# Level products of a chunked linear attention: 64-partition operands replaced by 128-partition ones, with each head's decayed queries beside zeros

## The chip, the cores and the metric

The kernel runs on one core of one Trainium2 chip. The metric is the device time of one launch, in microseconds (us), as the median of several runs. The engines are TensorE (PE in the profile, with PEld its weight loads), VectorE (DVE), ScalarE (ACT), GpSimd (POOL) and SyncE (SP), each with its own instruction stream; they meet at semaphores.

## The reference, cut to what matters

One layer of a hybrid decoder block on 512 tokens of width 2048: adaLN modulation, one input projection, three groups of heads (pooling, gated linear attention, sparse attention), an output projection, and a SwiGLU FFN. Only the gated linear attention matters here. It has 4 heads, keys of 64 and values of 128 elements:

```
bc = cumsum(log_a)                                   # decay, per token and key element
att[i,j] = sum_d q[i,d] * k[j,d] * exp(bc[i,d] - bc[j,d])     for j <= i
out = att @ v + (q * exp(bc)) @ state
```

The kernel works in chunks of 128 tokens. The exponent of a difference can't be split into a factor for the query and one for the key without overflow, so the kernel splits the causal triangle of a chunk into levels: the diagonal (level 0), and then for each half-size h of 64, 32, ..., 1 (levels 1 to 7) all pairs whose key lies in the first half and whose query lies in the second half of a block of 2h tokens. For such a pair the decay is taken relative to the last token of the first half, and both factors are below one.

## The kernel before, in words

All weights are read as fp32, split by ACT and POOL into a high and a low part, and multiplied in three passes (line 347). The input projection comes first, then the linear attention, the pooling, the sparse attention, the output projection and the FFN. No other matmuls are placed beside the linear attention: PE, DVE and ACT hand its work back and forth.

Queries and keys lie transposed in `qkT`, `[128, 4, 512]`: planes 0 and 1 are the queries and planes 2 and 3 the keys. A plane holds two heads, the first in partitions 0 to 63, the second in partitions 64 to 127. `bb[1]` holds the cumulated decay in the same layout.

For level l DVE computes two differences into `ee` (lines 1078, 1079), ACT takes their exponent in place (line 776), and DVE multiplies the keys of the first halves into `kd` (line 1096) and the queries of the second halves into `qd` (line 1097). Each is one instruction over 128 partitions and 512 elements; the other halves of `kd` and `qd` stay zero, as memsets at lines 1041 to 1044 left them. There are two `qd` and two `kd` buffers, used in turn. The semaphore `lev_qk` then releases PE, which computes 16 products of 128 x 128 (`level`, line 478), four to each of four PSUM banks, and counts `lev_att` after each bank. DVE copies each bank into `att` under the level's mask (`copies`, line 1068). Each fp32 matmul appears in the profile as two MATMUL records, so a level has 32. The four products of a bank all take the same 64 partitions; banks 0 and 2 take partitions 0 to 63, banks 1 and 3 take partitions 64 to 127.

The order on DVE's queue is: differences of level l, `copies(l - 1)`, in the first four levels the reduction of a squared-norm tile at line 1084 (which releases POOL's next two instructions, lines 301 and 302), then the products for `kd` and `qd` of level l. So each level's matmuls wait for the copies of the level before them, and these wait for its matmuls.

Behind the levels `qd[0]` and `kd[0]` are filled once more with full 128-token decays (lines 1106, 1107); PE transposes `kd[0]` (line 495) and runs the sums over values and states (lines 506, 510, 518).

Of the kernel before, what the change touches and what calls it, by code (L numbers as in the profile page):

```python
# [13 lines left out]
P = 128  # L14
D = 2048
S = 512
# [28 lines left out]
ALU = mybir.AluOpType  # L45
# [23 lines left out]
def layer_kernel(nc, x, wstream, mstream, vecs, rows, grow_bias, tabs, cmp_tab, up, pool_w, w1, w2, out):  # L69
    with ExitStack() as ctx:  # L70
# [5 lines left out]
        def at(name, shape, dt=F32, offset=None):  # L76
            size = int(np.prod(shape[1:])) * 4
            if offset is None:
                offset = place[0]
                place[0] += -(-size // 32) * 32  # L80
            assert offset + size <= 229344, name
            return nc.alloc_sbuf_tensor_at(name, shape, dt, offset=offset)
# [27 lines left out]
        qkT = at("qkT", [P, 4, S], F32, pbase + 4 * T * 4096)  # L110
# [11 lines left out]
        place[0] = abase  # L122
        bb = [at(f"bb{i}", [P, 2, S]) for i in range(2)]
        ee = [at(f"ee{i}", [P, 2, S]) for i in range(2)]
        qd = [at(f"qd{i}", [P, 2, S]) for i in range(2)]
        kd = [at(f"kd{i}", [P, 2, S]) for i in range(2)]
        att = at("att", [P, T * LH, P])
        kdN = at("kdN", [P, T, 2 * P])
        state = at("state", [P, 2, 2 * P])
# [55 lines left out]
        ps = ctx.enter_context(nc.psum_tensor("ps", [P, 8, U], F32))  # L185
# [15 lines left out]
        lev_e, lev_exp, lev_qk, lev_att, lev_cp = sem("lev_e"), sem("lev_exp"), sem("lev_qk"), sem("lev_att"), sem("lev_cp")  # L201
# [141 lines left out]
        def _(pe):  # L343
# [96 lines left out]
            for k in range(KD):  # L440
                if k % 4 == 0:
                    pe.wait_ge(unit_ready, U_LG + k // 4 + 1)
                col = slice((k % 4) * 64, (k % 4) * 64 + 64)
                ins = passes(ps[0:64, 4, :], hmH[:, k, :], hmL[:, k, :], whi[:, k // 4, col], wlo[:, k // 4, col],
                             False, k == 0, k == KD - 1)
# [18 lines left out]
            for f in range(2):  # L464
                ins = nc.tensor.matmul(ps[:, f, :], upw[0:16, f * P:(f + 1) * P], lgT[0:16, :], start=True, stop=True)
            ins.then_inc(pe_gla, 1)

            for t in range(T):
                ins = nc.tensor.transpose(ps[:, 5, t * 64:(t + 1) * 64], lgT[0:64, t * P:(t + 1) * P], ident[0:64, 0:64])
            ins.then_inc(pe_gla, 1)  # L470

            def level(l, q_, k_):

                for n in range(4):
                    p0 = (n % 2) * 64
                    for c in range(4):
                        tok = slice((2 * (n // 2) + c // 2) * P, (2 * (n // 2) + c // 2 + 1) * P)
                        ins = nc.tensor.matmul(ps[:, 4 * (l % 2) + n, c * P:(c + 1) * P], k_[p0:p0 + 64, c % 2, tok],  # L478
                                               q_[p0:p0 + 64, c % 2, tok], start=True, stop=True)
                    ins.then_inc(lev_att, 1)  # L480

            pe.wait_ge(dve_gla, 1)
# [10 lines left out]
            for t in range(T):  # L493
                for f in range(2):
                    ins = nc.tensor.transpose(ps[:, t // 2, (t % 2) * 256 + f * P:(t % 2) * 256 + (f + 1) * P],
                                              kd[0][:, f, t * P:(t + 1) * P], ident[:, :])
# [3 lines left out]
            for t in range(T):  # L500
                if t:
                    pe.wait_ge(st_ready, t)
                for f in range(2):
                    if t:

                        nc.tensor.matmul(ps[:, t, f * 256:(f + 1) * 256], qd[0][:, f, t * P:(t + 1) * P], state[:, f, :],
                                         start=True, stop=False)
                    for h in (2 * f, 2 * f + 1):
                        a_h = att[:, 8 * (t // 2) + 4 * (h % 2) + 2 * (t % 2) + f, :]
                        ins = nc.tensor.matmul(ps[:, t, h * P:(h + 1) * P], a_h,  # L510
                                               proj[:, t, 512 + h * P:512 + (h + 1) * P],
                                               start=t == 0, stop=t == 0 or h % 2 == 1)
                ins.then_inc(o_psum, 1)
                if t < T - 1:
                    for h in range(LH):
                        f, p0 = h // 2, (h % 2) * 64
                        v_h = proj[:, t, 512 + h * P:512 + (h + 1) * P]
                        ins = nc.tensor.matmul(ps[p0:p0 + 64, 4 + t, h * P:(h + 1) * P], kdN[:, t, h * 64:(h + 1) * 64],
                                               v_h, start=True, stop=True)
                    ins.then_inc(st_psum, 1)  # L520


            for g in range(4):
                pe.wait_ge(dve_gla, 3)
                u_g = slice(g * P, (g + 1) * P)
                for t in range(T):
                    first = ptab[:, 3 * g + (0 if t == 0 else 1), :]
                    ins = nc.tensor.matmul(ps[:, g, t * P:(t + 1) * P], proj[:, t, u_g], first, start=True, stop=t == 0)
                    if t:
                        ins = nc.tensor.matmul(ps[:, g, t * P:(t + 1) * P], proj[:, t - 1, u_g], ptab[:, 3 * g + 2, :],  # L530
                                               start=False, stop=True)
                ins.then_inc(pool_pe, 1)
            for g in range(4):
                pe.wait_ge(pool_act, g + 1)
                nc.tensor.matmul(ps[:, 4 + g, :], poolw[:, g * P:(g + 1) * P], poolD[:, g, :],
                                 start=True, stop=True).then_inc(pool_pe, 1)


            for v in range(2):
                pe.wait_ge(c_dup, v + 1)  # L540
                for g in range(G):
# [4 lines left out]
                    for t in range(T):  # L546
                        ins = nc.tensor.transpose(ps[:, g, t * P:(t + 1) * P], dup[:, t, g * P:(g + 1) * P], ident[:, :])
# [6 lines left out]
                for i in range(16):  # L554
                    pe.wait_ge(c_gt, 16 * v + i + 1)
                    for m in range(2):
                        ins = nc.tensor.matmul(ps[:, 4 + m, 0:P], w1s[:, i, m * P:(m + 1) * P], gt[:, i, :],  # L557
                                               start=i == 0, stop=i == 15)
                ins.then_inc(c_hid, 1)
                pe.wait_ge(c_hsaved, v + 1)  # L560
                if v == 0:
                    for m in range(2):
                        ins = nc.tensor.matmul(ps[:, 6, 0:DH], hid[:, m, :], w2s[:, 0, m, :], start=m == 0, stop=m == 1)
# [4 lines left out]
                else:  # L568
                    for g in range(G):
                        pe.wait_ge(c_act, g + 1)  # L570
                        for m in range(2):
                            ins = nc.tensor.matmul(ps[:, 6 + g % 2, 0:DH], hrep[:, m, :], w2s[:, 1, m, :],
                                                   start=m == 0, stop=m == 1)
# [5 lines left out]
            with pe.Fori(0, G) as g:  # L579
                pe.wait_ge(n_qk, g + 1)  # L580
                pe.wait_ge(o_saved, 4 * g + 4)
                for a in range(2):
                    for t in range(T):
                        ins = nc.tensor.transpose(ps[:, a, t * P:(t + 1) * P], qn[:, t, a * P:(a + 1) * P], ident[:, :])
                    ins.then_inc(n_tr, 1)
                for b in range(2):
                    for t in range(T):
                        ins = nc.tensor.transpose(ps[:, 3 + b, t * P:(t + 1) * P], kn[:, t, b * P:(b + 1) * P], ident[:, :])
# [48 lines left out]
                for n in range(NU):  # L637
                    t, r, b = units[n]
# [17 lines left out]
            for k in range(4, KD):  # L656
# [3 lines left out]
                for t in range(T):  # L660
                    ins = nc.tensor.transpose(ps[:, k % 8, t * P:(t + 1) * P], proj[:, t, c0:c0 + P], ident[:, :])
# [10 lines left out]
            for k in range(KD):  # L672
                if k >= 8:
                    pe.wait_ge(f_ready, k - 7)
                for t in range(T):
                    ins = nc.tensor.transpose(ps[:, k % 8, t * P:(t + 1) * P], xn[:, t, k * P:(k + 1) * P], ident[:, :])
# [270 lines left out]
        def _(dve):  # L947
# [90 lines left out]
                                   op0=ALU.mult, op1=ALU.min).then_inc(dve_gla, 1)  # L1038
            V.memset(att[:, :, :], 0.0)
            V.memset(state[:, :, :], 0.0)  # L1040
            V.memset(qd[0][:, :, :], 0.0)
            V.memset(qd[1][:, :, :], 0.0)
            V.memset(kd[0][:, :, :], 0.0)
            own(V.memset(kd[1][:, :, :], 0.0))

# [24 lines left out]
            for l, hs in enumerate(LEVELS, 1):  # L1070

                e = ee[l % 2][:, :, :].rearrange("p f s -> p (f s)").rearrange("p (n a s) -> p n a s", a=2, s=hs)
                b = bc.rearrange("p (n a s) -> p n a s", a=2, s=hs)
                nb = 2 * S // (2 * hs)
                ref = b[:, :, 0, hs - 1:hs].to_broadcast([P, nb, hs])
                if l >= 2:
                    dve.wait_ge(lev_qk, l - 1)
                V.tensor_tensor(e[:, :, 0, :], ref, b[:, :, 0, :], ALU.subtract)
                V.tensor_tensor(e[:, :, 1, :], b[:, :, 1, :], ref, ALU.subtract).then_inc(lev_e, 1)
                copies(l - 1)  # L1080
                if l <= T:

                    dve.wait_ge(qk_sq, l)
                    V.tensor_reduce(qr[:, (l - 1) * NH:l * NH], nsq[:, :].rearrange("p (h d) -> p h d", d=DH),
                                    AX.X, ALU.add).then_inc(qk_sum, 1)
                if l == T + 1:
                    dve.wait_ge(qk_sum, T)
                    V.tensor_scalar(qr[:, :], qr[:, :], 1.0 / DH, EPS, ALU.mult, ALU.add).then_inc(qk_var, 1)
                dve.wait_ge(lev_exp, l)
                if l >= 3:  # L1090
                    dve.wait_ge(lev_att, 4 * (l - 2) + 4)
                qv = qkT[:, 0:2, :].rearrange("p f s -> p (f s)").rearrange("p (n a s) -> p n a s", a=2, s=hs)
                kv = qkT[:, 2:4, :].rearrange("p f s -> p (f s)").rearrange("p (n a s) -> p n a s", a=2, s=hs)
                qo = qd[l % 2][:, :, :].rearrange("p f s -> p (f s)").rearrange("p (n a s) -> p n a s", a=2, s=hs)
                ko = kd[l % 2][:, :, :].rearrange("p f s -> p (f s)").rearrange("p (n a s) -> p n a s", a=2, s=hs)
                V.tensor_tensor(ko[:, :, 0, :], kv[:, :, 0, :], e[:, :, 0, :], ALU.mult)
                V.tensor_tensor(qo[:, :, 1, :], qv[:, :, 1, :], e[:, :, 1, :], ALU.mult).then_inc(lev_qk, 1)

            b = bb[1][:, :, :].rearrange("p f (t s) -> p (f t) s", t=T)
            e = ee[0][:, :, :].rearrange("p f (t s) -> p (f t) s", t=T)  # L1100
# [2 lines left out]
            V.tensor_tensor(e, b[:, :, P - 1:P].to_broadcast([P, 2 * T, P]), b, ALU.subtract).then_inc(lev_e, 1)  # L1103
            copies(7)
            dve.wait_ge(lev_exp, 8)
            V.tensor_tensor(qd[0][:, :, :], qkT[:, 0:2, :], ee[1][:, :, :], ALU.mult)
            V.tensor_tensor(kd[0][:, :, :], qkT[:, 2:4, :], ee[0][:, :, :], ALU.mult).then_inc(lev_qk, 1)
            for t in range(T - 1):
                dve.wait_ge(st_psum, t + 1)
# [307 lines left out]
```

## Time and profile before

| | us |
|---|---|
| median of 3 runs | 2764.28 (2763.25 to 2765.51) |
| the profiled execution, its own time | 2766.02 |
| its span, first to last instruction | 2764.2 |
| PE busy (share of the span) | 2541.9 (92%) |
| DVE busy | 1060.8 (38%) |
| ACT busy | 850.5 (31%) |
| POOL busy | 1057.2 (38%) |

PE's busy time counts overlapping records once. Line numbers are those of the kernel before. The granted clock (PEclk) is 1.00 at 2.4 GHz and 0.50 at 1.2 GHz.

### The profile page before, as it was taken

To read this page: it belongs to the slowest core of one execution; us is meant where nothing else is said; L and a number is where in the kernel's file an instruction comes from. 1 tells how busy PE (TensorE), PEld (TensorE's weight loads), DVE (VectorE), ACT (ScalarE), POOL (GpSimd) and SP (SyncE) were. 2 spreads that over 40 slices of the span, in tenths; PEclk is the share of its full clock that TensorE was granted. 3 is DMA by queue.
4 is the path that set the end of the run, shared out by engine and by line. 5 is a ranking of instruction groups with operands and counts; after the bars stand their busy time and mean duration, and the time that the engine had idled before them with its cause. 6 is when DMAs were issued, how large, how long until landed. Compare 5 with 4: busy or idle time off the path is not lost.

```text
span 2764.2 us, 35964 instructions
## 1 busy us (share of the span) xinstructions
PE 2541.9 (92%) x11497; PEld 2070.3 (75%) x11497; DVE 1060.8 (38%) x1626; ACT 850.5 (31%) x1571; POOL 1057.2 (38%) x816
## 2 busy tenths in 40 slices
PE   5699999956479999997999999999999999999998
PEld 4677778845367777876888888888888888888887
DVE  4756777767334552113131222222222313131404
ACT  3032222221255653323323222222222222222222
POOL 0034445521300002442444444444444444444444
PEclk9999999975778999998999999999999999999999
DMA  9837777720200003221222222222222222222233
GB/s 335 271 134 259 272 273 274 269 103 0 78 1 1 0 0 114 91 91 51 94 92 94 96 91 91 98 91 91 99 91 91 94 95 91 94 96 91 91 99 121
DMA packets 86615, 318.57 MB, mean 115 GB/s; under 512 B 9632, under 2 KB 10288, under 8 KB 85040
## 3 DMA queue, kind: packets, MB, share of 16 engines
q1 hardware_dynamic: 84672, 306.44, 32.5%
q10 hardware_dynamic: 1904, 11.62, 1.1%
q8 instruction: 24, 0.39, 0.1%
q14 instruction: 15, 0.12, 0.0%
HBM read 313.82 MB, written 4.19 MB: 115 GB/s over the span
## 4 chain that ended last, share of the span: by engine, by line
PE 89%; DVE 6%; ACT 2%; DMA 2%; issue 1%; ACTq 0%; DVEq 0%; SPq 0%
PE ps L347 75%; PE ps L597 3%; PE ps L626 3%; PE ps L615 1%; PE ps L478 1%; DMA modw<-in_mstream 1%; DVE macc L987 1%; PE ps L557 1%; DVE macc L989 1%; PE ps L604 1%; PE ps L410 1%; PE ps L401 1%; DMA xin<-in_x 0%; PE ps L394 0%; DVE dtmp L1281 0%
## 5 line engine op out<-in xcount | busy, mean ns | idle before, releaser
L289 POOL TENSOR_TENSOR wlo<-raw,whi 128x512 fp32r<-128x512 f32 x744 | 1004.0, 1350 | 1400.5 <-ACT whi L706 1400.5
L706 ACT ACTIVATE whi<-raw 128x512 fp32r<-128x512 f32 x744 | 469.7, 632 | 1493.8 <-PE ps L347 1488.9
L347 PE MATMUL ps<-hfH,whi 128*128 128x512 f32 x1408 | 559.4, 397 | 5.0 <-DVE hfull L1291 5.0
L347 PE MATMUL ps<-hfL,whi 128*128 128x512 f32 x1408 | 559.1, 397 | 0.0
L347 PE MATMUL ps<-hfH,wlo 128*128 128x512 f32 x1408 | 559.0, 397 | 0.0
L1307 DVE TENSOR_TENSOR hfull<-gsil,ps 128x512 f32<-128x512 f32 x44 | 30.3, 688 | 893.2 <-PE ps L347 449.9
L347 PEld LDWEIGHTS ps<-hfH,whi 128*128 128x128 f32 x1408 | 265.9, 189 | 70.2 <-DVE hfull L1291 5.4
L347 PEld LDWEIGHTS ps<-hfL,whi 128*128 128x128 f32 x1408 | 265.9, 189 | 64.7
L347 PEld LDWEIGHTS ps<-hfH,wlo 128*128 128x128 f32 x1408 | 265.8, 189 | 64.9
L347 PE MATMUL ps<-wlo,huH 128*128 128x512 f32 x704 | 280.8, 399 | 0.0
L347 PE MATMUL ps<-whi,huL 128*128 128x512 f32 x704 | 277.5, 394 | 0.0
L347 PE MATMUL ps<-whi,huH 128*128 128x512 f32 x704 | 276.1, 392 | 0.0
L969 DVE SCALAR_TENSOR_TENSOR macc<-modw,cact,macc 128x512 f32<-128x512 f32 x240 | 263.9, 1100 | 12.9 <-DMA modw<-in_mstream 3.1
L347 PE MATMUL ps<-whi,hmH 128*128 128x512 f32 x512 | 204.7, 400 | 0.0
L347 PE MATMUL ps<-wlo,hmH 128*128 128x512 f32 x512 | 204.1, 399 | 0.0
L347 PE MATMUL ps<-whi,hmL 128*128 128x512 f32 x512 | 201.9, 394 | 0.0
L1321 DVE TENSOR_TENSOR dtmp<-ps,grow 128x512 f32<-128x512 f32 x176 | 121.8, 692 | 205.6 <-PE ps L347 189.4
L1323 DVE TENSOR_TENSOR x<-x,dtmp 128x512 f32<-128x512 f32 x176 | 182.8, 1039 | 6.0
L347 PEld LDWEIGHTS ps<-whi,huL 128*128 128x128 f32 x704 | 132.1, 188 | 34.3
L347 PEld LDWEIGHTS ps<-whi,huH 128*128 128x128 f32 x704 | 132.2, 188 | 31.7
L347 PEld LDWEIGHTS ps<-wlo,huH 128*128 128x128 f32 x704 | 132.2, 188 | 30.5
L347 PEld LDWEIGHTS ps<-whi,hmL 128*128 128x128 f32 x512 | 96.1, 188 | 26.1 <-issue 1.9
(243 smaller groups left out, 2704.3 us busy)
## 6 DMA issues: line engine op xcount, KB each, us to landing
raw<-in_wstream SPq DMA_DIRECT2D x372, 512.0 KB, 3.3
modw<-in_mstream SPq DMA_DIRECT2D x192, 512.0 KB, 4.9
xin<-in_x SPq DMA_DIRECT2D x4, 1024.0 KB, 8.3
w1s<-in_w ACTq DMA_DIRECT2D x2, 2048.0 KB, 7.8
x<-in_x ACTq DMA_DIRECT2D x4, 1024.0 KB, 8.7
out_y<-x SPq DMA_DIRECT2D x16, 256.0 KB, 3.2
grow<-in_grow_bias SPq DMA_DIRECT2D x1, 2048.0 KB, 18.5
cmpb<-in_cmp_tab ACTq DMA_DIRECT2D x1, 1024.0 KB, 9.7
```

What stands on the lines that cost most here:

```text
L289: nc.gpsimd.tensor_tensor(wlo[:, s, :], raw[:, r, :], whi[:, s, :].bitcast(F32), ALU.subtract).then_inc(unit_ready, 1)
L347: ins = nc.tensor.matmul(acc, lhs, rhs, start=first and n == 0, stop=last and n == 2)
L401: ins = nc.tensor.matmul(ps[:, 4 + j, 0:1], macc[:, j * P:(j + 1) * P], ones[:, 0:1], start=j >= 2, stop=True)
L410: ins = nc.tensor.transpose(ps[:, k % 4, t * P:(t + 1) * P], xin[:, t, k * P:(k + 1) * P], ident[:, :])
L478: ins = nc.tensor.matmul(ps[:, 4 * (l % 2) + n, c * P:(c + 1) * P], k_[p0:p0 + 64, c % 2, tok], q_[p0:p0 + 64, c % 2, tok], start=True, st ...
L597: nc.tensor.matmul(ps[:, n % 3, 0:w], qT[:, r // 2, t * P:(t + 1) * P], kz[:, 2 * b + r % 2, 0:w], start=True, stop=True).then_inc(s_psum, 1)
L626: ins = nc.tensor.matmul(ps[:, 5 + t % 2, b * 256 + r * DH:b * 256 + (r + 1) * DH], pT[:, n % 2, c * P:(c + 1) * P], v_b, start=c == 0, st ...
L706: A(whi[:, k % SPLIT, :], raw[:, k % 8, :], ACT.Copy).then_inc(unit_hi, 1)
L969: ins = V.scalar_tensor_tensor(out=macc[:, :], in0=src, scalar=scal, in1=macc[:, :], op0=ALU.mult, op1=ALU.add)
L1307: V.tensor_tensor(hfull[:, c, :], gsil[:, c, :], ps[:, 4 * a + 2 + c, :], ALU.mult).then_inc(up_saved, 1)
L1321: own(V.tensor_tensor(dtmp[:, t % 2, :], ps[:, 4 * (c % 2) + t, :], grow[:, D + 512 * c:D + 512 * (c + 1)], ALU.mult))
L1323: V.tensor_tensor(x1[:, t, col], x1[:, t, col], dtmp[:, t % 2, :], ALU.add).then_inc(y_added, 1)
```

## The change

For levels 1 to 7 the queries get two buffers for each parity in place of one: `qd[i][0]` holds decayed queries in partitions 0 to 63 and zeros in 64 to 127, `qd[i][1]` the other way round. The product at line 1097 becomes two instructions over 64 partitions each. The matmuls of levels 1 to 7 take all 128 partitions of the keys and of one of the two query buffers; the zeros cancel the other head of the plane. Level 0 stays with 64 partitions. The memsets at the start clear four `qd` buffers in place of two, and the last full product of the queries goes to `bb[0]`, which is free by then.

```diff
-        qd = [at(f"qd{i}", [P, 2, S]) for i in range(2)]
+        qd = [[at(f"qd{i}{a}", [P, 2, S]) for a in range(2)] for i in range(2)]
...
-                        ins = nc.tensor.matmul(ps[:, 4 * (l % 2) + n, c * P:(c + 1) * P], k_[p0:p0 + 64, c % 2, tok],
-                                               q_[p0:p0 + 64, c % 2, tok], start=True, stop=True)
+                        if l == 0:
+                            lhs, rhs = k_[p0:p0 + 64, c % 2, tok], q_[p0:p0 + 64, c % 2, tok]
+                        else:
+                            lhs, rhs = k_[:, c % 2, tok], q_[n % 2][:, c % 2, tok]
+                        ins = nc.tensor.matmul(ps[:, 4 * (l % 2) + n, c * P:(c + 1) * P], lhs, rhs,
+                                               start=True, stop=True)
...
-                        nc.tensor.matmul(ps[:, t, f * 256:(f + 1) * 256], qd[0][:, f, t * P:(t + 1) * P], state[:, f, :],
+                        nc.tensor.matmul(ps[:, t, f * 256:(f + 1) * 256], bb[0][:, f, t * P:(t + 1) * P], state[:, f, :],
...
-            V.memset(qd[0][:, :, :], 0.0)
-            V.memset(qd[1][:, :, :], 0.0)
+            for i in range(2):
+                for a in range(2):
+                    V.memset(qd[i][a][:, :, :], 0.0)
...
-                V.tensor_tensor(qo[:, :, 1, :], qv[:, :, 1, :], e[:, :, 1, :], ALU.mult).then_inc(lev_qk, 1)
+                for a in range(2):
+                    half = slice(a * 64, (a + 1) * 64)
+                    ins = V.tensor_tensor(qo[a][half, :, 1, :], qv[half, :, 1, :], e[half, :, 1, :], ALU.mult)
+                ins.then_inc(lev_qk, 1)
...
-            V.tensor_tensor(qd[0][:, :, :], qkT[:, 0:2, :], ee[1][:, :, :], ALU.mult)
+            V.tensor_tensor(bb[0][:, :, :], qkT[:, 0:2, :], ee[1][:, :, :], ALU.mult)
```

## Rows read from the trace of the kernel before

**Rows 1.** The page: the chain that ended last, by engine.

```profile
PE 89%; DVE 6%; ACT 2%; DMA 2%; issue 1%; ACTq 0%; DVEq 0%; SPq 0%
```

**Rows 2.** The chain in time (start us, us, what): before the levels.

```profile
597.01 0.67 DVE qd L1041
...
598.09 0.91 DVE qd L1042
...
599.16 0.91 DVE kd L1043
...
600.24 0.92 DVE kd L1044
601.18 1.24 DVE bb L1047
```

**Rows 3.** The chain in time: matmuls of levels 1, 2, 6 and 7.

```profile
620.31 5.14 PE ps L478 x32
...
630.78 5.15 PE ps L478 x32
...
664.38 5.14 PE ps L478 x32
...
669.59 0.58 issue
670.17 0.68 DVE kd L1096
670.85 0.61 DVE qd L1097
...
671.50 5.14 PE ps L478 x32
```

**Rows 4.** Timeline of POOL and DVE, 576 to 622 us (start us, us, engine, line, op).

```profile
578.16 1.89 POOL L301 TENSOR_TENSOR nsq<-proj 128x1024 f32<-128x1024 f32 x1
...
617.87 2.38 DVE L1097 TENSOR_TENSOR qd<-qkT,ee 128x512 f32<-128x512 f32 x1
620.29 1.41 DVE L1078 TENSOR_TENSOR ee<-bb 128x512 f32<-128x512 f32 x1
621.62 0.68 DVE L1079 TENSOR_TENSOR ee<-bb 128x512 f32<-128x512 f32 x1
...
617.43 2.27 POOL L301 TENSOR_TENSOR nsq<-proj 128x1024 f32<-128x1024 f32 x1 [36.39 <-DVE qr L1084]
619.67 1.48 POOL L302 TENSOR_TENSOR nsq<-proj 128x512 f32<-128x512 f32 x1
```

**Rows 5.** Timeline of DVE: the copies of one level.

```profile
673.61 0.73 DVE L1068 COPY_PREDICATED att<-gmask,ps 128x512 f32<-128x512 uint32 x1 [0.83 <-PE ps L478]
674.63 0.73 DVE L1068 COPY_PREDICATED att<-gmask,ps 128x512 f32<-128x512 uint32 x1 [0.29 <-PE ps L478]
```

**Rows 6.** Timeline of PE: 128-partition fp32 records of 128 x 128.

```profile
745.53 3.19 PE L557 MATMUL ps<-gt,w1s 128*128 128x128 f32 x14
...
748.30 3.89 PE L557 MATMUL ps<-gt,w1s 128*128 128x128 f32 x32
```

**Rows 7.** Stretches: from:to us, PE, PEld, DVE, ACT, POOL busy, PEclk, DMA share, GB/s.

```profile
646.22:649.62 3.40, 0.15 (x1) 0.00 (x0) 3.21 (x4) 0.00 (x0) 0.00 (x0) 1.00 0.00 0
657.20:676.70 19.50, 15.39 (x96) 14.51 (x96) 14.26 (x23) 4.22 (x5) 0.00 (x0) 0.50 0.00 1
679.60:690.50 10.90, 8.34 (x35) 6.96 (x36) 1.19 (x5) 4.56 (x7) 0.00 (x0) 0.50 0.00 0
690.60:704.20 13.60, 5.50 (x43) 4.38 (x41) 3.42 (x9) 3.63 (x6) 0.00 (x0) 1.00 0.00 1
720.90:724.70 3.80, 3.73 (x17) 3.73 (x18) 0.02 (x1) 0.34 (x1) 0.00 (x0) 0.50 0.00 0
724.75:734.90 10.15, 7.95 (x49) 5.68 (x47) 1.11 (x3) 4.75 (x8) 5.46 (x11) 1.00 0.13 24
762.10:765.60 3.50, 3.47 (x16) 3.27 (x16) 0.00 (x0) 2.21 (x4) 0.00 (x0) 0.50 0.00 0
```

More of the change, by code:

```diff
@@ L1093, in _ @@
                 kv = qkT[:, 2:4, :].rearrange("p f s -> p (f s)").rearrange("p (n a s) -> p n a s", a=2, s=hs)
-                qo = qd[l % 2][:, :, :].rearrange("p f s -> p (f s)").rearrange("p (n a s) -> p n a s", a=2, s=hs)
+                qo = [qd[l % 2][a][:, :, :].rearrange("p f s -> p (f s)").rearrange("p (n a s) -> p n a s", a=2, s=hs)
+                      for a in range(2)]
                 ko = kd[l % 2][:, :, :].rearrange("p f s -> p (f s)").rearrange("p (n a s) -> p n a s", a=2, s=hs)
                 V.tensor_tensor(ko[:, :, 0, :], kv[:, :, 0, :], e[:, :, 0, :], ALU.mult)
-                V.tensor_tensor(qo[:, :, 1, :], qv[:, :, 1, :], e[:, :, 1, :], ALU.mult).then_inc(lev_qk, 1)
+                for a in range(2):
+                    half = slice(a * 64, (a + 1) * 64)
+                    ins = V.tensor_tensor(qo[a][half, :, 1, :], qv[half, :, 1, :], e[half, :, 1, :], ALU.mult)
+                ins.then_inc(lev_qk, 1)
             b = bb[1][:, :, :].rearrange("p f (t s) -> p (f t) s", t=T)
```

## The prediction

> **What bounds the kernel now.** I read the page first: PE holds 89% of the chain that ended last [rows 1], but that is a share over all stages, and this change touches one of some 100 us. So I read the chain in order of time there. Each late level is the same sequence: 32 matmul records in 5.14 us, the end of the last copy of their result (0.6 us), the key product, the query product, and the next 32 records [rows 3]. PE and DVE take turns, and neither hides anything of the other: DVE's next products stand in its queue behind the copies, which wait for PE. From start to start of level 6 and 7 it is 7.12 us. Level 0 (same form, unchanged) runs under the memsets and is off the path. Levels 1 to 7 are on it: seven groups of 5.14 us, 36 us in all. The memsets of `qd` and `kd` are on it as well: each starts about 1.075 us after the one before it, and the first decay instruction follows the last of them without a gap [rows 2]. Nothing behind the stage has slack that I can see: the later stages wait for its results in turn, so I let each microsecond pass through to the end at full price.
>
> **Memsets.** The change adds two of 128 x 1024. Price 1.075 us each, from 597.01 to 599.16 for two [rows 2]; no cover, since ACT's exponents of `ee`, which the decay instruction also needs, end before the memsets do. **+2.15 us.**
>
> **The split query product.** One instruction becomes two over half of the partitions, with as many elements per partition. The trace shows no product like it. If half the partitions cost half the time, the two cost what the one did (+0); if only the elements per partition count, each costs what the whole did. All steps of DVE here go by elements per partition (128 x 1024 at 0.91 as a memset, 128 x 512 at 0.61 on the path), and I take the second: +0.61 us in levels 4 to 7 [rows 3], **+2.4 us** for four.
>
> Levels 1 to 3 are another matter. Their query product takes 2.38 us, not 0.68, and the difference instruction behind it 1.41 [rows 4]. POOL starts its two squares at the same moment, as the reduction before the products releases them; they take 2.27 and 1.48 us there, against 1.89 for the first when DVE was idle. The two engines hold each other up. The DVE instruction in the second place, now the difference, is off the path, because PE works meanwhile. With the change the second query product stands in that place, ahead of PE's release: it takes the 1.33 us from 620.29 to 621.62. The difference comes later, undelayed, and is still hidden under PE's first bank. I take 1.33 us for three levels, **+4.0 us**; the bounds are 0 and 3 x 1.41 = 4.2.
>
> **The matmuls.** Columns do not change, so one could price this at nothing. But look at the spacing. At the low clock, 14 records over 128 partitions take 3.19 us from first start to last end [rows 6], and a record that is alone in that stretch lasts about 0.42 us: (3.19 - 0.42) / 13 = 0.213 us from start to start. At 0.213, 32 records with a slower first one (0.37 us to the second) would take 0.37 + 30 x 0.213 + 0.42 = 7.2 us. The level takes 5.14 at the same low clock [rows 3, 7]. DVE's copies show where the difference comes from: a bank's 8 records would be 1.71 us apart, yet copies after the first start 1.02 us apart, each released by PE [rows 5]. Neighbouring banks use different halves of the array's rows, and their matmuls run partly side by side. With operands of 128 partitions no two can. At the low clock this costs 7.2 - 5.14 = 2.06 us a level, 14.4 us for seven.
>
> The Trainium skill has this rule too: TensorE: Matmul & The Clock Gate, Part 3, says that matmuls in different row groups run concurrently and that a small contraction alone takes as long as a full one. TensorEngine Tiling gives up to 2x for a contraction of at most 64; by that a full level would be estimated at 10.3 us and seven would cost 36 us more. The rows above give a ratio of 1.4 (7.2 to 5.14), and the sum goes by them.
>
> Against this stands the clock. The last three levels ran wholly at 0.50, and so did the others; only behind the third it stood at 1.00 for 3.4 us, while PE was all but idle, and it was gone before the fourth [rows 7]. Full-height work raised it sooner: PE started at 720.97 from idle and the clock was 1.00 from 724.7 on; transposes from 762.13 had it after some 3.5 us. In the stage of 679.6, with pauses, it took until 690.5 [rows 7]. So I expect the clock to rise within a level of over 5 us, and the rest of its records to run at the high rate: 32 records in 3.89 us [rows 6], about 0.116 each, 0.097 less than at the low clock. A rise 3.5 us into the level leaves 16 records, which gives 7.2 - 1.6 = 5.6 us; one at 4.2 us leaves 13 and gives 5.9; none gives 7.2; high from the start gives 3.9. I take 5.9, as these levels start in pauses of more or less than the stretches I read from: 5.9 - 5.14 = 0.76, seven times, **+5.3 us**. By the next level the clock has fallen again: the pause (2.0 us before and 2.6 with the second product; in the first levels 5.3 and 6.7) [rows 3] is as idle as that after the third level.
>
> **Elsewhere nothing.** The last query product only changes its target. The later stages are moved by some 14 us, and some of their clock rises may fall a little differently; +-2 us, taken as zero.
>
> **Sum.** 2.15 + 2.4 + 4.0 + 5.3 = +13.9 us. The profiled execution took 2766.0 us, 1.8 of it outside the span, and becomes 2779.9. The median of the runs is 1.7 below it: 2764.3 + 13.9 = **2778.2 us**.
>
> **Rivals.** (A) *The clock stays low through all levels.* For: the 15 us of PE work from 657.2 to 676.7 didn't raise it [rows 7]. Against: that was half-height work, and the full-height stretches above all did. Then 14.4 in place of 5.3: 2787.3.
> (B) *Once up, the clock stays up from level 4 on.* For: from 690.6 to 704.2 it stayed at 1.00 with PE busy 5.5 of 13.6 us [rows 7]. Against: the fall after level 3. Levels 5 to 7 then take 3.9 in place of 5.9: 2772.2.
> (C) *The high clock holds from the first level through the stage behind them*: the end on the other side. Each level is 1.24 us below 5.14 (-8.7), and the stage of 679.6 to 690.5, with 8.34 us of PE at 0.50 [rows 7], gives back up to half of it (-4.2). Against the +8.55 of DVE that is -4.3: 2760. It decides at the level's price: below 3.9 us on average even the levels alone pay for DVE's work. Against it: pauses of 6 us in the first three levels.
> (D) *The side-by-side running is not a matter of rows*: 128-partition levels would also take 5.14 us or less at the low clock. Then DVE's +8.55 and a little clock gain: 2771. The two spacings at one clock speak against it [rows 5, 6], and so does the page's rule.
>
> **How the numbers follow.** The forecast case has 0.68, with its own range 2771 to 2784 (rise at 3.4 to 6 us into a level; the second product at 0 to full price). A 0.12, B 0.10, C 0.04, D 0.06. The range reaches down to B and below it, to 2769, and up to A, 2787. A measurement of this kernel can tell 0.2% (5.5 us) from no change. Slower by more than that: the forecast case, A, B and nearly all of D, 0.92 with some reserve. Within it: half of C and some unforeseen cover, 0.05. Faster: 0.03.
>
> **What would show it.** In the changed kernel's profile: two products of about 0.68 us at 64 x 512 per level, the second at 1.4 or so in levels 1 to 3, with the difference of line 1078 back at 0.69 there; six memsets at 1.075; 32 records per level in 5.5 to 6.7 us, banks 1.7 us apart at first and 0.9 at the end; PEclk at 1.00 in a part of each level. Wrong if a level takes 5.1 or less with the clock at 0.50 (D), if the clock is at 1.00 at a level's start (B, C), or if copies or products are no longer on the path.

## The result and the profile after

The changed kernel takes 2771.33 us as the median of 9 runs (2770.37 to 2773.33), the kernel before 2763.57 in the same comparison: a ratio of 1.0028, 95% interval 1.0017 to 1.0038. It is 7.8 us slower. The forecast was 13.9 us slower, 2778.2 us; 2771.33 lies in the range (2769 to 2787), 2.3 us above its lower end, and the change cost little more than half of what was forecast. The profiled execution of the changed kernel took 2771.24 us with a span of 2769.5.

The line numbers of the changed kernel are a little higher: the memsets of `qd` are at 1047, the key and query products at 1102 and 1105, the level matmuls at 482.

The chain in time of the changed kernel (start us, us, what): the gate bias, the memsets, level 1, the matmuls of levels 2 to 7, the transposes, the first sum over states, and ACT's squares.

```profile
590.86 1.42 DVE bb L1038 x2
...
596.37 0.67 DVE qd L1047
...
597.44 0.91 DVE qd L1047
...
598.52 0.91 DVE qd L1047
...
599.59 0.91 DVE qd L1047
...
619.46 2.29 DVE qd L1105
...
621.77 1.45 DVE qd L1105
...
623.26 5.63 PE ps L482 x32
...
635.67 6.22 PE ps L482 x32
...
648.67 6.54 PE ps L482 x32
...
658.18 0.59 DVE qd L1105
...
658.79 0.70 DVE qd L1105
...
659.53 6.24 PE ps L482 x32
...
668.56 5.19 PE ps L482 x32
...
676.42 3.85 PE ps L482 x32
...
682.95 3.85 PE ps L482 x32
...
689.84 1.11 PE ps L499 x8
...
696.54 0.70 PE ps L510 x2
...
707.16 2.07 ACT gsq L793 x4
```

The same places of the kernel before that no row above shows:

```profile
591.50 1.42 DVE bb L1034 x2
...
679.69 1.99 PE ps L495 x8
...
687.26 1.22 PE ps L506 x2
...
699.41 2.06 ACT gsq L789 x4
```

Read against [rows 2, 3], this is most of the account of the stage. Two more memsets at 1.075 us. In level 1 a second query product of 1.45 us where the difference instruction stood before, in level 4 one of 0.70. And seven groups of 32 matmul records, none at 5.14: four above 5.6, one at 5.19, two at 3.85. Behind the levels, the transposes and the first sum over states are shorter than before. The granted clock says why. Stretches of the changed kernel (columns as in [rows 7]):

```profile
635.60:638.50 2.90, 2.83 (x13) 2.83 (x14) 2.03 (x4) 1.06 (x1) 0.00 (x0) 0.50 0.02 6
...
659.50:663.00 3.50, 3.47 (x16) 3.47 (x17) 2.02 (x3) 1.06 (x1) 0.00 (x0) 0.50 0.00 0
...
672.40:689.60 17.20, 9.02 (x76) 8.44 (x75) 15.86 (x23) 3.16 (x4) 0.00 (x0) 1.00 0.00 1
```

Levels 2 and 4 begin at 0.50 and speed up before they end. So does level 5. From level 5's second half to the transposes at 689.84 the clock is at 1.00 without a break, though PE is busy for only 9.0 of the 17.2 us of the last line. DVE's copies of level 4 show the rise inside a level:

```profile
661.65 0.72 DVE L1073 COPY_PREDICATED att<-gmask,ps 128x512 f32<-128x512 uint32 x1 [0.84 <-PE ps L482]
663.36 0.72 DVE L1073 COPY_PREDICATED att<-gmask,ps 128x512 f32<-128x512 uint32 x1 [0.98 <-PE ps L482]
664.90 0.73 DVE L1073 COPY_PREDICATED att<-gmask,ps 128x512 f32<-128x512 uint32 x1 [0.83 <-PE ps L482]
665.80 0.72 DVE L1073 COPY_PREDICATED att<-gmask,ps 128x512 f32<-128x512 uint32 x1 [0.16 <-PE ps L482]
```

The second bank is 1.71 us behind the first (8 records at 0.213; it was 1.02 in [rows 5]), the last 0.90 us behind the third.

**Two parts of the time.** For each profiled execution the chain gives the start of the gate bias (line 1034 of the kernel before) and of ACT's squares behind the levels (line 789). Between them lies the stage; the rest is what follows. Before: 591.50 to 699.41, 107.9 us. After: 590.86 to 707.16, 116.3 us. So the stage lost 8.4 us, while the time from the squares to the end of the span fell from 2064.8 to 2062.3. Over all eleven profiled executions of this study that second part lay between 2061.6 and 2066.4 us, although its instructions are the same in all. The granted clock goes with it: in the first 120 us behind the squares it was 0.67 in the four profiles with 2065.5 us and more, 0.69 in the two with 2064.8 and 2065.0, and 0.70 to 0.73 in the five with 2061.6 to 2062.4. Whether that clock belongs to the kernel or only to the execution can't be told from one profile of each, so a difference of 2 us there is not put down to the change.

### The profile page after: what moved, and what is told of

It reads as the page before. It is cut to its first block, busy times and chain, and to the rows that moved or that the text cites. A ratio compares the mean times of both kernels' runs of the same rounds, so it can differ in the third digit from the quotient of the medians.

```text
span 2769.5 us, 35973 instructions
## 1 busy us (share of the span) xinstructions
PE 2537.2 (92%) x11497; PEld 2067.0 (75%) x11497; DVE 1069.1 (39%) x1635; ACT 849.8 (31%) x1571; POOL 1057.1 (38%) x816
## 4 chain that ended last, share of the span: by engine, by line
PE 88%; DVE 6%; ACT 2%; DMA 2%; issue 1%; ACTq 0%; DVEq 0%; SPq 0%
PE ps L347 75%; PE ps L601 3%; PE ps L630 2%; PE ps L619 1%; PE ps L482 1%; DMA modw<-in_mstream 1%; DVE macc L991 1%; PE ps L561 1%; DVE macc L993 1%; DVE qd L1105 1%; PE ps L608 1%; PE ps L410 1%; PE ps L401 1%; DMA xin<-in_x 0%; PE ps L394 0%
## 5 line engine op out<-in xcount | busy, mean ns | idle before, releaser
L973 DVE SCALAR_TENSOR_TENSOR macc<-modw,cact,macc 128x512 f32<-128x512 f32 x240 | 263.9, 1100 | 13.3 <-DMA modw<-in_mstream 3.5
```

The costliest lines, as they stand in the source:

```text
L973: ins = V.scalar_tensor_tensor(out=macc[:, :], in0=src, scalar=scal, in1=macc[:, :], op0=ALU.mult, op1=ALU.add)
```

## The experiments

Each kernel was timed in 3 rounds against the kernel before. The medians of the kernel before were 2764.65 (first four), 2764.33 (next four) and 2764.09 (last). A ratio is formed from all runs and need not be the quotient of the two medians.

### The matmuls alone

This kernel leaves out the zeros beside a head's queries.

```diff
-                        ins = nc.tensor.matmul(ps[...], k_[p0:p0 + 64, c % 2, tok],
-                                               q_[p0:p0 + 64, c % 2, tok], start=True, stop=True)
+                        rows = slice(p0, p0 + 64) if l == 0 else slice(0, P)
+                        ins = nc.tensor.matmul(ps[...], k_[rows, c % 2, tok],
+                                               q_[rows, c % 2, tok], start=True, stop=True)
```

> The kernel before with one edit: the matmuls of levels 1 to 7 take all 128 partitions of kd and qd. There are no zeros beside a head's queries, so the two heads of a plane are summed in att; this part of the computation is wrong, its instructions are those of the changed kernel on PE and those of before on DVE. Main theory (neighbouring banks no longer run side by side, but full-height work raises the clock): levels of 5.2 to 6.6 us where the clock rises inside and 3.9 where it is high from the start, together 37 to 38 us against 36.0; the stage behind the levels about 2.4 us shorter; in all -4 to 0 us against the kernel before. Rival (all of the +8 us of the change comes from the matmuls): 2771. Rival (128 partitions alone, clock unmoved): +14 us, levels of 7.2 us.

Measured: 2761.15 us, ratio 0.9999 (0.9988 to 1.0009). The ten runs fall into two groups, six at 2759.42 to 2761.81 us and four at 2766.30 to 2769.64, and the profile is of one of the six (2759.54). No difference from the kernel before that can be told, and in any case not +8. The timeline of PE (levels 1 to 7) has six levels between 5.18 and 5.95 us and one at 3.84:

```profile
618.30 5.95 PE L479 MATMUL ps<-qd,kd 128*128 128x128 f32 x32 [22.45 <-DVE qd L1098]
629.60 5.45 PE L479 MATMUL ps<-qd,kd 128*128 128x128 f32 x32 [5.34 <-DVE qd L1098]
...
664.25 3.84 PE L479 MATMUL ps<-qd,kd 128*128 128x128 f32 x32 [1.99 <-DVE qd L1098]
670.08 5.47 PE L479 MATMUL ps<-qd,kd 128*128 128x128 f32 x32 [1.99 <-DVE qd L1098]
```

The seven sum to 36.8 us against 36.0, and the whole stage takes 106.4 us against 107.9. In this profile the loss from no longer running side by side is paid back by the clock. DVE's instructions are those of before, so the change's loss is not in the matmuls.

### The DVE side alone

Against the changed kernel:

```diff
-                        if l == 0:
-                            lhs, rhs = k_[p0:p0 + 64, c % 2, tok], q_[p0:p0 + 64, c % 2, tok]
-                        else:
-                            lhs, rhs = k_[:, c % 2, tok], q_[n % 2][:, c % 2, tok]
+                        q_h = q_ if l == 0 else q_[n % 2]
+                        lhs, rhs = k_[p0:p0 + 64, c % 2, tok], q_h[p0:p0 + 64, c % 2, tok]
```

> The changed kernel, but the level matmuls read only their head's 64 partitions again: the DVE side of the change alone. Main theory: memsets +2.15, second products +0.7 in levels 4 to 7 and +1.4 in levels 1 to 3, together +9.2 us against the kernel before (2773), every level 5.14 us at 0.50. Rival (most of the +8 us is PE's): +4 us or less.

Measured: 2770.93 us (six runs, 2767.94 to 2775.48), ratio 1.0030 (1.0018 to 1.0043): not to be told from the whole change. The DVE terms were as expected, in level 1 for instance:

```profile
618.54 2.30 DVE qd L1103
620.85 1.45 DVE qd L1103
```

The +9.2 did not arrive in full: by the medians it was +6.3, in the stage of the profile +5.9 (113.8 us for 107.9). And "every level 5.14 us at 0.50" was a miss: the last levels took less.

```profile
655.46 5.13 PE L480 MATMUL ps<-qd,kd 64*128 64x128 f32 x32 [4.34 <-DVE qd L1103]
663.39 4.94 PE L480 MATMUL ps<-qd,kd 64*128 64x128 f32 x32 [2.80 <-DVE qd L1103]
671.01 4.39 PE L480 MATMUL ps<-qd,kd 64*128 64x128 f32 x32 [2.69 <-DVE qd L1103]
```

In the last two levels the clock was at 1.00 in a part of each. So half-height work can be followed by a rise as well; in this study that came later and less often than with full-height work. The changed kernel's stage is 2.5 us longer than this one's, so in these profiles the full-height matmuls gave nothing back.

### Fewer and more changes of the row half

Fewer, in `level` and in the same order in `copies`:

```diff
-                for n in range(4):
+                for n in (0, 2, 1, 3):
```

> The kernel before with the banks of a level in the order 0, 2, 1, 3, so that half-height matmuls change the row half once per level in place of three times. Main theory (the time is won where neighbours use different halves): about 0.69 us lost per dropped change of half, levels of about 6.5 us, +9 to +10 us in all. Rival (half-height matmuls are quick by themselves): levels of 5.14 us, no change.

More:

```diff
-                for n in range(4):
-                    p0 = (n % 2) * 64
-                    for c in range(4):
+                for m in range(2):
+                    for c in range(4):
+                        for a in range(2):
+                            p0 = a * 64        # bank 2 * m + a
```

> The kernel before with the matmuls of banks 0 and 1 taken in turns, and those of 2 and 3, so that the row half changes with each matmul. Main theory: nearly every matmul runs beside its neighbour, a level takes 3.7 to 4.2 us at the low clock; but banks come in pairs, and DVE's last copy ends some 5.2 us after the start in place of 5.8, so -3 to -5 us in all. Rival (overlap only at the change of a bank): levels of 5.14 us, 0 us. Rival (a change of half costs a drain): levels above 6 us, slower.

Measured: 2771.98 (ratio 1.0026, 1.0016 to 1.0035) and 2758.12 (0.9977, 0.9968 to 0.9987). In the stage that is +10.0 and -5.0 us (117.9 and 102.9 for 107.9), as expected; the medians moved by +7.3 where 9 to 10 was expected and by -6.5 where -3 to -5 was, the rest lying outside the stage. The timelines of PE, first that of the kernel with the order 0, 2, 1, 3:

```profile
620.33 6.50 PE L478 MATMUL ps<-qd,kd 64*128 64x128 f32 x32 [20.83 <-DVE qd L1097]
```

and that of the alternating kernel:

```profile
619.63 3.79 PE L479 MATMUL ps<-qd,kd 64*128 64x128 f32 x32 [23.54 <-DVE qd L1100]
```

The stretches over all levels of the first kernel, and of the second up to 669.1, have PEclk 0.50:

```profile
593.00:686.00 93.00, 51.76 (x256) 49.68 (x256) 72.22 (x89) 14.94 (x15) 11.15 (x6) 0.50 0.00 0
```

```profile
592.30:669.10 76.80, 29.27 (x250) 27.21 (x252) 69.26 (x88) 14.30 (x15) 11.15 (x6) 0.50 0.00 1
```

One clock, the same 32 records over 64 partitions: 6.50 us with one change of half, 5.13 with three, 3.79 with fifteen. Each of the two changes between the first two kernels saves 0.69 us; carried on to no change, which no run has, that gives the 7.2 us of the full height. That the 5.14 us comes from the order of the halves, as the forecast had it, is shown, and rival D refuted. The Trainium skill, TensorE: Matmul & The Clock Gate, Part 3, has matmuls in different row groups running concurrently; by that rule the alternating level should come near half of 7.2 us, by estimate 3.6, and the trace's 3.79 us agrees.

### The clock held up by filler matmuls

```diff
+                if l >= 2:
+                    pe.wait_ge(lev_cp, 4 * (l - 1))
+                    for m in range((0, 0, 22, 22, 14, 8, 8, 8)[l]):
+                        nc.tensor.matmul(ps[:, 4 * (l % 2), 0:P], ident[:, :], ones[:, :], start=True, stop=True)
                 pe.wait_ge(lev_qk, l)
```

Eight more of these fillers stand before the transposes behind the levels.

> The changed kernel with matmuls that nobody reads (128 partitions, ident by ones) in PE's pauses before levels 2 to 7 and before the transposes behind them: 22, 22, 14, 8, 8, 8 and 8. They end before the level is released if the clock is high. Main theory (a level costs 3.85 us at 1.00 and only the clock makes it more): levels 2 to 7 at 3.85 us in place of 6.2, 6.5, 6.2, 5.2, 3.85 and 3.85, so about -8 us against the changed kernel, level with or a little faster than the kernel before: 2760 to 2764. Rival (128-partition levels cost over 5 us at either clock, or the fillers only delay the levels): 2771 or more.

Measured: 2766.69 us (2760.42 to 2771.91), ratio to the kernel before 1.0008 (0.9998 to 1.0017); 4.6 below the changed kernel's median. The timeline of PE:

```profile
623.27 5.88 PE L482 MATMUL ps<-qd,kd 128*128 128x128 f32 x32 [26.02 <-DVE qd L1109]
...
635.96 3.84 PE L482 MATMUL ps<-qd,kd 128*128 128x128 f32 x32 [1.90 <-DVE qd L1109]
...
646.61 5.46 PE L482 MATMUL ps<-qd,kd 128*128 128x128 f32 x32 [1.90 <-DVE qd L1109]
...
656.43 3.84 PE L482 MATMUL ps<-qd,kd 128*128 128x128 f32 x32 [1.23 <-DVE qd L1109]
```

Five of the six filled levels take 3.84 us. In level 3 the clock was at 0.50 from about 648.1 to 651.5, behind a pause of 1.9 us that level 2 had too without harm, and that level took 5.46. The levels sum to 30.5 us against 37.5 in the changed kernel, and the stage is 5.6 us shorter (590.88 to 701.57). The median is 2.7 us above the top of what was expected: level 3 kept 1.6 us, and the part behind the squares was 2.7 us longer than in the changed kernel's profile. That a 128-partition level is worth 3.85 us at 1.00 and that only the clock makes it more is shown.

### The reduction moved, and the memsets moved

The reduction of line 1084 (its line in the kernel before), with its wait, goes ahead of `copies(l - 1)` in the changed kernel:

```diff
+                if l <= T:
+                    dve.wait_ge(qk_sq, l)
+                    V.tensor_reduce(qr[:, (l - 1) * NH:l * NH], ...).then_inc(qk_sum, 1)
                 copies(l - 1)
-                if l <= T:
-                    dve.wait_ge(qk_sq, l)
-                    V.tensor_reduce(qr[:, (l - 1) * NH:l * NH], ...).then_inc(qk_sum, 1)
```

> The changed kernel with the squared-norm reduction of levels 1 to 4 ahead of the copies, under PE's level, in place of behind them; POOL's two squares then start before the products. Main theory (the products of levels 1 to 3 take 3.74 us for 1.30 only because POOL runs beside them; the reduction's 1.63 us is on the path in levels 2 to 4): up to -2.4 us for three levels and -1.6 us for three, -9 to -12 us against the changed kernel, about 2760. Rival (the long products are due to their 64 partitions): only the reduction's -5 us.

Then the memsets too:

```diff
             dve.wait_ge(proj_saved, 36)
+            V.memset(att[:, :, :], 0.0)        # and state, qd, kd: all of them
             dve.wait_ge(pe_gla, 1)
```

> As the last, and the memsets of att, state, qd and kd in DVE's pause of 13 us before the gate projection arrives. Main theory: the 2.15 us of the two added memsets vanish, and 3.5 us more, down to where ACT's logarithm is ready: -5.7 us against the kernel with the early reduction, about 2754. The DVE price of the change is then only the second products, 0.7 us a level. Rival (ACT or the decay chain is the bound at once): -2 us or less.

Measured: 2761.61 (ratio 0.9987, 0.9978 to 0.9997), 9.7 us below the changed kernel as expected (13.3 in the stage of the profile), and 2753.16 (0.9966, 0.9952 to 0.9981). In the chain of the kernel with the early reduction, the query products of level 1 take 1.30 us in place of 3.74, with the same operands; the key product ahead of them now takes some of POOL's hold, 1.06 for 0.60:

```profile
620.25 1.06 DVE kd L1102
621.32 0.60 DVE qd L1105
621.92 0.70 DVE qd L1105
```

Here POOL's squares start at 617.88, before the products. So the long products were POOL's doing, not that of 64 partitions. With the memsets early, the first decay instruction starts 6.16 us behind the gate bias in place of 11.83, the 5.7 us expected. The 8.4 us between the two medians is more than that; in the two profiles the stretch from the last level's end to the squares differs by 3.2 us, as one had the transposes at 0.50 (1.97 us) and the other at 1.00 (1.10).

### Both moves in the kernel before

> The kernel before with the early reduction and the early memsets: the control to the changed kernel with both (2753.2 measured). Main theory: on the path -3.5 us for the memsets, -1.6 for the reduction in levels 2 to 4 and -1.2 for POOL's hold on the products in levels 1 to 3 (the key product keeps 0.45 of it, as in the changed kernel with both), -12 us in all, 2752; so with the DVE price down to 0.7 us a level the change costs 0 to +3 us, because its matmuls give back about what its second products take. Rival (the change is a loss of 8 us in any surrounding): 2745. Rival (the change becomes a gain): 2757 or more.

Measured: 2748.49 us, ratio 0.9945 (0.9928 to 0.9962), 3.5 us better than expected; against it the changed kernel with the same two moves is 4.7 us slower (2753.16), where 0 to 3 was expected. In the two profiles, however, the stage takes the same time, 93.8 us and 93.9 (591.51 to 685.34 and 591.86 to 685.78), and of the 4.4 us between the spans 4.0 lie in the part behind it, where the clock of the first 120 us was 0.73 in one and 0.67 in the other. So how much of the change's loss is left here is open, between nothing and 5 us. Where the 12 us was too small: the last level took 4.14 us, and in levels 2 and 3 both the reduction and the whole hold of POOL left the path (1.63 + 1.72 each), as the matmuls of 5.1 us cover both. The timeline of PE has the first four levels 7.12 apart, where levels 1 and 2 were 10.5 apart in [rows 3]:

```profile
615.59 5.13 PE L478 MATMUL ps<-qd,kd 64*128 64x128 f32 x32 [17.48 <-DVE qd L1097]
622.71 5.13 PE L478 MATMUL ps<-qd,kd 64*128 64x128 f32 x32 [1.99 <-DVE qd L1097]
```

### All three in the kernel before

> The kernel before with row halves alternating by matmul, the early reduction and the early memsets. Main theory: -6.5 for the alternation as measured, -3.5 for the memsets, and -5 to -9 for the reduction and POOL's squares, less than in the changed kernel, as a level of 3.8 us hides less than the reduction and four copies: 2746 to 2750, the fastest of all. Rival (the three hide behind each other, so that DVE becomes the bound): 2754 or more.

Measured: 2747.56 us, ratio 0.9942 (0.9925 to 0.9958), the fastest of the study, 16.8 us below the kernel before. The rival is partly true, though: beside both moves, alternation gains 0.9 us by the medians (of four runs each), not 6.5. The stage says more, 89.1 us for 93.8, but the part behind it was 4.2 us longer; what alternation is worth here is open, between 1 and 5 us. In the timeline of DVE for level 2 nothing waits for PE any more:

```profile
621.12 0.69 DVE L1081 TENSOR_TENSOR ee<-bb 128x512 f32<-128x512 f32 x1
621.73 0.68 DVE L1082 TENSOR_TENSOR ee<-bb 128x512 f32<-128x512 f32 x1
622.33 1.75 DVE L1086 TENSOR_REDUCE qr<-nsq 128x24 f32<-128x1536 f32 x1
623.99 2.54 DVE L1071 COPY_PREDICATED att<-gmask,ps 128x512 f32<-128x512 uint32 x4
626.42 1.17 DVE L1099 TENSOR_TENSOR kd<-qkT,ee 128x512 f32<-128x512 f32 x1
```

The four copies run back to back, and the 7.1 us from level 1 to 2 and from 2 to 3 is now DVE's own work, as long as without alternation. From level 3 on the levels follow each other at 6.0 to 6.6 us, where it was 7.0 to 7.2.

## Why the prediction was right, and where its sizes were off

The direction was earned, the total in part lucky. DVE's work came 0.65 us dearer than forecast, the levels 3.8 us cheaper, the work behind them 2.4 us cheaper. The result lies in the range because that reached down for rival B. The total alone can't tell the forecast case, whose own range began at 2771, from B (2772) or D (2771); the traces do.

**Direction and mechanism: right.** The kernel is slower because DVE's added work is all on the path and the matmuls give nothing back for it. The two halves run alone show both sides: ratios of 1.0030 for DVE's and 0.9999 for PE's.

**Memsets: right**, 2.15 us.

**Second query product: right, slightly low.** Levels 4 to 7 lost 0.69 us each, not 0.61: the second product costs 0.70 on the path. Together 2.8 for 2.4.

**POOL's hold in levels 1 to 3: right, slightly low.** 1.43 us a level for 1.33, so 4.3 for 4.0. The kernel with the early reduction shows the mechanism: 1.30 for 3.74 us. DVE in all: +9.2 for +8.55.

**The matmuls: right in kind, too dear.** The step that was mis-sized is "I take 5.9", seven times. Levels 1 to 4 took 5.63, 6.22, 6.54 and 6.24, on average 6.16, even a little more. But "By the next level the clock has fallen again" failed for the last levels: it rose within level 5 and stayed, and levels 6 and 7 took 3.85. The levels sum to 37.5 us, so +1.5 where +5.3 was forecast. That is rival B with a start one level later, and the forecast's own sign of being wrong, the clock at 1.00 at a level's start. The forecast held the fall after level 3 of the kernel before against B. Why the clock stayed here is open. Full-height work ahead of the pause is not enough: the pause of 2.80 us before level 5 had it too, and level 5 began at 0.50, while the one of 2.69 before level 6 kept the clock. In the kernel with the matmuls alone the pauses before levels 6 and 7 are both 1.99 us, and the levels took 3.84 and 5.47.

**Elsewhere nothing: wrong by 2.4 us in the stage.** With the clock still up, the eight transposes took 1.11 us for 1.99. The sums over values behind them were at 0.50 and no shorter than before, but from the first sums over states on it was at 1.00 again, 0.70 us for 1.22: from the last level's end to the squares 20.4 us where it was 22.8. Memsets 2.15, products 7.1, levels 1.5, less 2.4: 8.35, against 8.39 measured in the stage.

The rivals A (clock low throughout), C (clock high throughout) and D are refuted by the changed kernel: its clock was neither low nor high throughout, and at 0.50 its banks were 1.71 us apart. The two orders of banks speak against D as well.

## What to carry to other kernels

Operands of half the array's height are not a waste where neighbouring matmuls use different halves: ordering them so that the halves alternate took a group from 5.13 to 3.79 us at an unchanged clock, without an added instruction. Before trading such overlap for a higher clock, price the vector work that pads the operands, and ask which slot it takes: here the second product stepped into the one in which POOL held DVE up, and cost 1.43 us a level for 0.69. And once a wait is shortened, look for what else can go under it; moving two things whose results nobody needed yet took 15.6 us off the kernel before, twice the change's loss, and from level 1 to level 3 it left the better matmul order nothing to win, since DVE was then the bound.

## What the runs showed of the hardware that was not expected

The clock stayed at 1.00 for 17.2 us in which PE was busy for 9.0 us with pauses of 2.7 to 3.1 us; in the kernel before every level began at 0.50. In the kernel with fillers one pause of 1.9 us was followed by a fall and another was not, so the length of a pause alone does not tell. And identical instructions behind the squares took between 2061.6 and 2066.4 us in eleven profiled executions, more than half of what this change moved, the longer times at the lower clock.
